# Moving the norm and bonus products of a channel group between the half tiles of the next group, and handing the chunk buffers over from DVE, in a hybrid decoder block

## The reference

```python
p = xn @ w_in                                     # 3328 columns
c_b, c_c, c_h, p_rwkv = split(p)                  # 3 x 512 for the convolution, the rest for RWKV
y_conv = c_b * causal_dwconv(c_c * c_h, conv_w)
q = token_shift(p_rwkv, mu_shift)
r, k, v, d_w, d_a, d_g = split(q)                 # 3 x 512, 64, 64, 128
decay = exp(-exp(-softplus(-(w0 + tanh(d_w) @ w_decay_up)) - 0.5))
iclr = sigmoid(a0 + d_a @ w_iclr_up)
kk = k * k_k;  kk = kk / maximum(norm(kk, per head), 1e-12)
k = k * (1 + (iclr - 1) * k_a)
y = rwkv7_scan(r, decay, k, v, -kk, kk * iclr)    # recurrence over tokens, 8 heads of 64
...
y = groupnorm(y) + sum(r * k * r_k, per head) * v # the "bonus"
h = x + concat([y_conv, y * g]) @ w_out
y = rms_norm(h + moe_ffn(rms_norm(h)))            # 32 experts, top 4
```

## Time and profile before

| | us |
|---|---|
| median of 3 runs | 2707.74 (2706.63 to 2709.28) |
| the profiled execution | 2712.24, with a span of 2710.7 |
| projection of groups 1 to 3, from one decay product to the next (three stretches) | 57.04, 57.53, 57.78 |
| last tile of group 3 to the last bonus product | 166.51 |
| last bonus product to the first matmul of the chunks | 13.00 |
| chunks, post-processing and routing, to 1010 us | 553 |
| experts and last norm, behind it | 1700 |

### The profile page before, as it was taken

How to read it: one execution, slowest core, us unless ns; L and a number is a source line. 1 busy time by engine, 2 the same in 40 slices (tenths; PEclk the granted TensorE clock), 3 DMA queues, 4 the chain that set the end, 5 groups by cost and what they waited for, 6 DMA issues and landing times.

```text
span 2710.7 us, 52128 instructions
## 1 busy us (share of the span) xinstructions
PE 2465.5 (91%) x21408; PEld 2107.3 (78%) x21409; DVE 902.8 (33%) x2166; ACT 497.1 (18%) x1081; POOL 303.7 (11%) x343
## 2 busy tenths in 40 slices
PE   7999997788758939999999999999999999999993
PEld 4333444777724528999999999999999999999993
DVE  2556312555533642222222222222222222222222
ACT  3223001111231311112111111111111111111112
POOL 0000000000000230111111111111111111111110
PEclk9999998999878959999999999999999999999996
DMA  3101111110162226687787888778788888787863
GB/s 119 39 31 39 47 53 36 40 39 26 32 254 85 96 103 206 228 279 272 246 290 269 274 281 274 242 257 274 250 274 281 274 278 279 250 275 270 273 202 142
DMA packets 259303, 506.88 MB, mean 187 GB/s; under 512 B 23312, under 2 KB 39952, under 8 KB 259248
## 3 DMA queue, kind: packets, MB, share of 16 engines
q1 hardware_dynamic: 240224, 463.10, 48.6%
q0 software_dynamic: 19040, 43.24, 6.4%
HBM read 462.21 MB, written 38.90 MB: 185 GB/s over the span
## 4 chain that ended last, share of the span: by engine, by line
PE 66%; DVE 2%; DMA 1%; issue 1%; ACT 1%; POOL 0%; SPq 0%; POOLq 0%; DVEq 0%; ACTq 0%
PE ps L1331 37%; PE ps L1347 18%; PE ps L1259 4%; PE ps L1300 1%; PE ps L1310 1%; PE ps L1303 1%; PE ps L1313 1%; DMA arena<-normw 1%; PE ps L1284 1%; PE ps L1244 0%; PE ps L1248 0%; DVE arena L1022 0%; DMA arena<-wgate 0%; POOL list_s L461 0%; PE ps L1274 0%
## 5 line engine op out<-in xcount | busy, mean ns | idle before, releaser
L1331 PE MATMUL ps<-arena 128*128 128x136 f32 (+1 forms) x8192 | 1009.5, 286 | 13.7 <-issue 11.1
L1331 PEld LDWEIGHTS ps<-arena 128*128 128x128 f32 x8192 | 1003.1, 197 | 21.1 <-issue 21.1
L1347 PE MATMUL ps<-arena 128*128 128x136 f32 (+1 forms) x4096 | 506.2, 284 | 0.0
L1347 PEld LDWEIGHTS ps<-arena 128*128 128x128 f32 x4096 | 496.2, 190 | 1.3
L1029 PE MATMUL ps<-arena 128*128 128x512 f32 x832 | 363.5, 597 | 0.0
L987 DVE TENSOR_SCALAR arena<-ps,arena 128x160 f32<-128x160 f32 x256 | 98.2, 384 | 668.4 <-PE ps L1331 668.4
L1029 PEld LDWEIGHTS ps<-arena 128*128 128x128 f32 x832 | 158.8, 192 | 203.6 <-issue 203.6
L674 ACT ACTIVATE arena<-arena 128x160 f32<-128x160 f32 x256 | 86.1, 336 | 941.4 <-DVE arena L987 941.4
L1005 DVE TENSOR_SCALAR arena<-ps,idx_s 128x512 f32<-128x512 f32 x64 | 48.0, 750 | 511.5 <-PE ps L1310 511.5
L678 ACT ACTIVATE arena<-ps,arena 128x160 f32<-128x160 f32 x256 | 100.9, 394 | 427.2 <-PE ps L1347 427.2
L505 POOL DMA_INDIRECT sum_s<-arena,idx_s x32 | 53.5, 1671 | 1072.0 <-DVE arena L1007 1037.8
(11 more groups left out here) (222 smaller groups left out, 1899.6 us busy)
## 6 DMA issues: line engine op xcount, KB each, us to landing
arena<-gu_w SPq DMA_DIRECT2D x128, 2048.0 KB, 8.1
arena<-dn_w SPq DMA_DIRECT2D x64, 2048.0 KB, 7.7
arena<-w_in_t SPq DMA_DIRECT2D x26, 512.0 KB, 3.3
arena<-arena SPq DMA_DIRECT2D x32, 256.0 KB, 2.8
arena<-x SPq DMA_DIRECT2D x4, 1024.0 KB, 9.2
arena<-w_out SPq DMA_DIRECT2D x1, 4096.0 KB, 19.3
arena<-x SPq DMA_DIRECT2D x8, 512.0 KB, 5.8
xn_s<-arena SPq DMA_DIRECT2D x8, 512.0 KB, 2.7
```

Source lines behind the costliest of these rows:

```text
L1331: last = nc.tensor.matmul(ps[:, f % 2, k * C:k * C + size], wslot[u][:, kt, o:o + 2 * P - 1:2], xT[:, kt, 0:size], start=kt == 0, stop=kt ...
L1347: last = nc.tensor.matmul(ps[:, 2 + d % 2, 0:size], wslot[u][:, ft, d % 4 * P:(d % 4 + 1) * P], actT[:, ft, 0:size], start=ft == 0, stop=f ...
```

## The change

PE: in groups 1 to 3 the norm product of the group before goes between the halves of tile n (where the bonus product was), and the bonus product goes between the halves of tile n + 1. The first pass of the convolution's loop is written out, with the norm product of group 3 behind its first tile and the bonus product behind its second. The thresholds on `s_pm` follow (four small functions). The bonus product waits, besides for `s_rk`, until ACT has read the decay product from banks 6 and 7; the decay product waits for the square roots instead of for `bonus_product`, and the iclr product waits for `bonus_product`.

ACT: the square root of group i - 1 stands ahead of `copy_raw(n)` of group i, not at the end of its own group.

DVE: the shift of the v tile stands ahead of the wait for the square root, and `bonus_product(i - 1)` behind the scan of group i. The last one stands ahead of the convolution loop.

Border: POOL writes all four bonus blocks ahead of the convolution's results. DVE sets `s_z` when its last convolution product is made, and POOL waits for it. SP waits for the convolution's writes only ahead of the post-processing inputs. The semaphores of the last stage's loads are shared with those of x.

```diff
+        def decay_products(i):
+            return 8 * i - 2 if i else 0
+        def iclr_products(i):
+            return 8 * i + 2 if i else 2
+        def norm_products(i):
+            return 8 * i + 4
+        def bonus_products(i):
+            return 8 * i + 8 if i < RT - 1 else 8 * i + 6
...
+            sp.wait_ge(s_cvr, RT + 1)
             for i in range(RT):
                 sp.dma_start(bonus_in[:, i, :], bonus_d[i]).then_inc(s_pi, 16)
...
-            for i in range(RT - 1):
+            for i in range(RT):
                 pool.wait_ge(s_bu, i + 1)
                 pool.dma_start(bonus_d[i], bonus_st[:, i % 2, :]).then_inc(s_bo[i % 2], 16)
+            for k in range(2):
+                pool.wait_ge(s_bo[k], 16 * RT // 2)
             with pool.Fori(0, RT) as i:
...
-            pool.wait_ge(s_bu, RT)
-            pool.dma_start(bonus_d[RT - 1], bonus_st[:, (RT - 1) % 2, :]).then_inc(s_bo[(RT - 1) % 2], 16)
-            for k in range(2):
-                pool.wait_ge(s_bo[k], 16 * RT // 2)
-            pool.sem_inc(s_z, 2)
+            pool.wait_ge(s_z, 2)
...
+            def norm_root(i):
+                for h in range(2):
+                    act.wait_ge(s_pm, norm_products(i) + h + 1)
+                    nc.scalar.activation(W8[:, h * HALF:(h + 1) * HALF], ps[:, 6 + h, :], ACT.Sqrt).then_inc(s_nr, 1)
             for i in range(RT):
                 n = 2 + 3 * i
+                if i:
+                    norm_root(i - 1)
                 copy_raw(n)
                 for h in range(2):
-                    act.wait_ge(s_pm, 8 * i + h + 1)
+                    act.wait_ge(s_pm, decay_products(i) + h + 1)
                     if h == 0 and i:
                         act.wait_ge(s_td, i)
...
-                for h in range(2):
-                    act.wait_ge(s_pm, 8 * i + 4 + h + 1)
-                    nc.scalar.activation(W8[:, h * HALF:(h + 1) * HALF], ps[:, 6 + h, :], ACT.Sqrt).then_inc(s_nr, 1)
+            norm_root(RT - 1)
...
             for i in range(RT):
                 n = 2 + 3 * i
-                if i:
-                    bonus_product(i - 1)
                 shift(n, q_r)
...
                 nc.vector.tensor_tensor(W1, W2, W1, ALU.subtract).then_inc(s_cu, 1)
+                if i:
+                    bonus_product(i - 1)
                 shift(n + 1, q_k)
...
+                shift(n + 2, V[:, i, :])
                 dve.wait_ge(s_nr, 2 * i + 2)
...
-                shift(n + 2, V[:, i, :])
+            bonus_product(RT - 1)
...
-            bonus_product(RT - 1)
-
+            dve.wait_ge(s_cd, 2 * RT + 1)
+            dve.sem_inc(s_z, 2)
             lo, hi = slice(0, N), slice(N, P)
-            dve.wait_ge(s_z, 2)
...
             def bonus(i):
+                pe.wait_ge(s_rk, i + 1)
+                if i + 1 < RT:
+                    pe.wait_ge(s_sg, 4 * (i + 1) + 2)
+                else:
+                    pe.wait_ge(s_nr, 2 * RT)
...
             for i in range(RT):
                 n = 2 + 3 * i
-                tile(n, bonus(i - 1) if i else None)
+                tile(n, (lambda: norm(i - 1)) if i else None)
                 pe.wait_ge(s_lo, 1)
-                if i:
-                    pe.wait_ge(s_bu, i)
                 for h in range(2):
+                    if i:
+                        pe.wait_ge(s_nr, 2 * i + h - 1)
                     nc.tensor.matmul(ps[:, 6 + h, :], lora[0:LORA, i * P:(i + 1) * P],
                                      tdwa[0:LORA, h * HALF:(h + 1) * HALF], start=True, stop=True).then_inc(s_pm, 1)
-                tile(n + 1)
+                tile(n + 1, (lambda: bonus(i - 1)) if i else None)
+                if i:
+                    pe.wait_ge(s_bu, i)
...
+            conv_tile(0, 0)
+            norm(RT - 1)
+            conv_tile(0, 1)
+            bonus(RT - 1)
+            conv_tile(0, 2)
+            with pe.Fori(1, RT) as i:
                 for j in range(3):
-            bonus(RT - 1)()
+                    conv_tile(i, j)
```

More of the change, by code:

```diff
@@ L222, in build @@
         GROUPS = TT // GROUP
-        s_x = [sem(f"x_in{g}") for g in range(4)]
+        s_x = [sem(f"x_then_sums_in{g}") for g in range(4)]
         s_par = sem("params_in")
@@ L296, in build @@
         s_dn, s_dd, s_yt, s_ye, s_l1 = sem("dn"), sem("dn_copied"), sem("y_by_token"), sem("y_rows"), sem("lin")
-        s_md, s_yl = sem("experts_done"), [sem(f"sums_in{g}") for g in range(4)]
+        s_md = sem("experts_done")
         s_fi, s_o, s_out = sem("final_inputs"), sem("out_ready"), two("written")
@@ L565, in _ @@
                 for h in range(2):
-                    act.wait_ge(s_pm, 8 * i + 2 + h + 1)
+                    act.wait_ge(s_pm, iclr_products(i) + h + 1)
                     nc.scalar.activation(W4[:, h * HALF:(h + 1) * HALF], ps[:, 6 + h, :], ACT.Sigmoid,
@@ L685, in _ @@
                 for t in range(g * GROUP, (g + 1) * GROUP):
-                    act.wait_ge(s_yl[g], 16)
+                    act.wait_ge(s_x[g], 32)
                     act.wait_ge(s_sq2, TT + t)
@@ L742, in bonus_product @@
             def bonus_product(i):
-                dve.wait_ge(s_pm, 8 * i + 8)
+                dve.wait_ge(s_pm, bonus_products(i) + 2)
                 if i >= 2:
@@ L1042, in bonus @@
             def bonus(i):
[L1043 to L1048, removed]
+                pe.wait_ge(s_rk, i + 1)
[3 more added lines that the diff above has]
+                    pe.wait_ge(s_nr, 2 * RT)
+                for h in range(2):
+                    nc.tensor.matmul(ps[:, 6 + h, :], ones2, W8[:, h * HALF:(h + 1) * HALF],
+                                     start=True, stop=True).then_inc(s_pm, 1)
             def transpose_x(t):
@@ L1078, in _, with norm @@
                 project(n, ring_pair(n), 1).then_inc(s_pj, 1)
+            def norm(i):
+                pe.wait_ge(s_sk, i + 1)
+                for h in range(2):
+                    pe.wait_ge(s_sg, 4 * i + 2 + h + 1)
+                    nc.tensor.matmul(ps[:, 6 + h, :], ones2, W8[:, h * HALF:(h + 1) * HALF],
+                                     start=True, stop=True).then_inc(s_pm, 1)
             for i in range(RT):
                 n = 2 + 3 * i
-                tile(n, bonus(i - 1) if i else None)
+                tile(n, (lambda: norm(i - 1)) if i else None)
                 pe.wait_ge(s_lo, 1)
+                for h in range(2):
+                    if i:
+                        pe.wait_ge(s_nr, 2 * i + h - 1)
+                    nc.tensor.matmul(ps[:, 6 + h, :], lora[0:LORA, i * P:(i + 1) * P],
+                                     tdwa[0:LORA, h * HALF:(h + 1) * HALF], start=True, stop=True).then_inc(s_pm, 1)
+                tile(n + 1, (lambda: bonus(i - 1)) if i else None)
                 if i:
                     pe.wait_ge(s_bu, i)
-                for h in range(2):
-                    nc.tensor.matmul(ps[:, 6 + h, :], lora[0:LORA, i * P:(i + 1) * P],
-                                     tdwa[0:LORA, h * HALF:(h + 1) * HALF], start=True, stop=True).then_inc(s_pm, 1)
-                tile(n + 1)
                 for h in range(2):
@@ L1093, in _, with conv_tile @@
                 tile(n + 2)
-                pe.wait_ge(s_sk, i + 1)
+            def conv_tile(i, j):
+                pe.wait_ge(s_wcv[j], 16 * i + 16)
                 for h in range(2):
[L1096 to L1099, removed]
-                for j in range(3):
[L1101 to L1110, removed]
-            bonus(RT - 1)()
+                    if j == 0:
+                        pe.wait_ge(s_ccp, 2 * i + 1)
+                        pe.wait_ge(s_pc, 2 * NR)
+                    elif j == 1:
+                        pe.wait_ge(s_u, 2 * i + 1)
+                    else:
+                        pe.wait_ge(s_cd, 2 * i + 1)
+                    project((NR + j) % 3, ring_pair(NR + j), h).then_inc(s_pcv, 1)
+            conv_tile(0, 0)
[4 more added lines that the diff above has]
+            with pe.Fori(1, RT) as i:
+                for j in range(3):
+                    conv_tile(i, j)
             heads = [(r, h) for r in range(RT) for h in range(2)]
```

2 lines of the change are left out of this document (1 added, 1 removed).

## The result

The changed kernel takes 2782.81 us (median of 4 runs, 2782.22 to 2784.57), before 2707.18 in the same comparison: a ratio of 1.028, 95% interval 1.0266 to 1.0294. It is 76 us slower where 19 us faster were forecast. The profiled execution took 2782.22 with a span of 2780.7, 70.0 more than the span before.

A forecast was written before the change was run, and what follows sets the result against it. PE, busy 91% of the span, was taken as the bound. Group waits and low clock 25.7, less new waits 7.2, clock 3.4 and convolution 0.8, plus border 4.5, gave 18.8 us: 2707.7 to 2688.9 us, range 2683 to 2695.

The forecast's parts named there:

- The new wait: Ahead of the bonus product in groups 1 to 3, PE waits 2.4 us each for ACT's sigmoid, 7.2 in all.
- Behind tile 13: The convolution's first tile waits for the last raw copy and starts late: 0.8 us lost.
- Low clock: PE's clock falls behind two of the three new waits, 1.7 us each, 3.4 us lost.
- The border: Last convolution matmul to first chunk matmul takes 6.8 us; 4.5 us gained (4.2 to 5.5).
- the sum: All terms over the groups, convolution and border together: 18.8 us gained.
- rival (4): 48 more matmuls in PE's code add pauses for code, 6.24 us each; four give 2713.9 us; chance 0.02.
- the stages behind shift as a whole: The stages after the border start earlier by the gain and otherwise stay as they were.
- The last sign that the prediction names for being wrong: In the chunk stage: the forecast is wrong if the chunks' own passes change their length; no size given.
- (1): Behind the short waits in the groups the clock doesn't fall: 22.2 us gained, 2685.5 us; chance 0.17.
- (2): First chunks wait for something other than SP's start, border gives nothing: 14.3 us gained, 2693.4 us; chance 0.06.
- (3): In the groups, late roots and three clock falls cost 14.4 us: 15.0 gained in all, 2692.7 us; chance 0.11.

The follow-up runs named there:

- e5: e3 with one DVE instruction, the last reader of W1 with its signal, moved ahead of three others: 2676.74 us, ratio 0.9891.
- e1: The changed kernel with 53 empty semaphore increments at the head of PE's program, no work moved: 2687.81 us, ratio 0.993.
- e8: The changed kernel with 100 empty PE instructions at the head: 2691.21 us (1 run).
- e9: The changed kernel with 113 empty PE instructions at the head: 2694.0 us (1 run).
- e11: The changed kernel with 163 empty PE instructions at the head: 2792.71 us (1 run).
- e3: The changed kernel without the written-out convolution pass, group 3's norm product ahead of the loop and bonus product behind it: 2684.55 us, ratio 0.9917.
- e4: The kernel before with only the first pass of PE's convolution loop written out, nothing moved: 2799.41 us, ratio 1.0345.
- e6: The changed kernel with 53 empty PE instructions behind the chunk loop instead of at the head: 2736.22 us (1 run).
- e7: The changed kernel with 20 empty PE instructions at the head: 2734.0 us (1 run).
- e2: The kernel before with 203 empty instructions at the head of PE's program and nothing else: 2822.51 us, ratio 1.0431.

## Why the prediction was wrong

**Right, by its terms.** The new wait, forecast at 2.4 us in each of three groups: 2.40 in the trace, three times, with the forecast releaser. Behind tile 13: 0.8 forecast, 0.77 measured. Low clock: I took two falls in three waits; there is one, behind the first wait (the half tile at 134.34 takes 8.29 us instead of 7.03), so 1.7 us less were lost than forecast. The Trainium skill (TensorE: Matmul & The Clock Gate, Why this matters for your kernels) asks for no gaps over about 3 us. By that none of the three waits should have cost clock; the trace agrees at two of them and not at the first, all of 2.40 us. The border: 6.8 us from the last convolution matmul to the first chunk matmul, and 7.2 measured (430.52 by DVE's row at 430.72 less 0.20, to 437.75). The 0.4 are in the write that now runs beside the fetches: from the first fetch to the first chunk matmul it is 5.99 us, 1.4 more than before, where 1.0 was taken and 1.3 was the bound.

That the sum came out to the tenth, 18.8 us, is in part luck. Against the 1.7 us of the fall that didn't come stand 0.4 at the border, 0.4 by a later start of this execution (73.53 against 73.12), and 0.7 by which the three waits cost more than their idle time: from decay product to decay product a group takes 48.85 us in e5, without a wait, and 51.48 in the changed kernel with a wait and no fall (173.85 to 225.33), so a wait costs 2.63. Where the code's place is put right (e1), the whole kernel takes 2687.8 against the 2688.9 predicted.

**Wrong: rival (4) and the sentence "the stages behind shift as a whole".** The step that failed is the pricing of longer PE code. I named code as the one thing that could turn the sign, but took it for a number of single pauses, 6.24 us each at the entry of a loop body, asked only how many of them the 48 new matmuls would add, and gave that a chance of 0.02. The runs show in its place a property of the loops that come after: they run without new fetches or they don't, depending on where they begin. In the chunk loop a bad place costs in every pass, 45.3 us in eight. In the experts it is indeed single pauses, five of 7.1 to 7.6 us, but they come where the loop changes from one body to the other, 900 us and more behind the added code; that stage lost 43.5. The length of what was added decides nothing by itself: 203 instructions more cost 89 us, 256 none (e1), 303 and 316 none (e8, e9), 366 again some 90 (e11). My "against" for the rival, that PE ran straight-line code up to 443.57 without a pause, was beside the point, and only in part true: behind the groups that stretch is the convolution's loop, of some 200 instructions, with no pause either. The last sign that the prediction names for being wrong, that the chunks' own passes change their length, is the one that came.

What could have been read before: the trace of before has 27 code packets in all, six in the first chunk pass and none in the other seven, so this loop, 1710 instructions of the 2048 that the Trainium skill's figure (Advanced Engine Details and Errata, ISA Cache) would allow, repeats without a fetch, and there is little to spare. And comparing the two programs' PE instructions ahead of it gives the shift. Both facts together don't say on which side of the border the new place falls, so a fair forecast would have been two cases, 2689 and about 2780, near even.

**Other rivals.** (1) no fall of the clock: one came. (2) the border gives nothing: refuted, 4 us came. (3) late square roots: refuted, L778's counterpart starts at 114.61, 2.6 us behind the norm product.

## What to carry to other kernels

When a change lengthens or shortens the program ahead of a big loop of PE, compare the instruction queue's packet count (part 3 of the page) before and after, and take the loops' place as a variable of its own: a few empty instructions in an idle stretch put it back (53 here). Idle time for "issue" in a loop whose code wasn't touched is the sign to look for. To judge a reordering, compare it at a restored place (e1, e3), or its gain or loss is that of the place.

## What the hardware showed that I had not expected

- Writing out one pass of a loop, 48 matmuls, costs 93 us in stages that start later (e4), and 53 empty instructions win 95 back (e1).
- The effect is two-valued for each loop, and one loop can be good while the other is bad (e6, e7).
- In the experts the cost comes only where the loop changes bodies: five pauses of 7.1 to 7.6 us in the changed kernel, each ahead of the second expert of size 136 behind one of size 160.
- The clock fell behind one of three waits of 2.40 us that look alike, in the changed kernel behind the first, in e3 and e1 behind the second.
- An empty semaphore increment on PE isn't free: 203 of them delayed the chunks by 19.5 us, though they stood in an idle stretch of 11.8 us (e2). The 53 of e1 moved them by 0.3.
